# Two-sided mixers: the first output projection moved ahead of the ninth pair's scores, ten warm-up products for eight, and a small load moved ahead of the first weights

## What is computed

```python
for l in range(DEPTH):                      # DEPTH = 2, SEQ = 256, D_MODEL = 1024
    h = rms_norm(x, ffn1_norm[l])
    x = x + 0.5 * swiglu(h, ffn1_w_gate[l], ffn1_w_up[l], ffn1_w_down[l])
    h = rms_norm(x, mix_norm[l])
    (na_q, na_k, na_v, df_q, df_k, df_v,
     gq_q, gq_k, gq_v, dl_q, dl_k, dl_v) = split_in_proj(h @ w_in[l])
    ...
    o = jnp.concatenate([o_a, o_b, o_c, o_d], axis=-1)
    x = x + o @ w_out[l]
    h = rms_norm(x, ffn2_norm[l])
    x = x + 0.5 * swiglu(h, ffn2_w_gate[l], ffn2_w_up[l], ffn2_w_down[l])
```

## Time and profile before

| | us |
|---|---|
| median of 3 runs (lowest to highest) | 1570.04 (1569.96 to 1570.6) |
| the profiled execution, its own time | 1568.18 |
| its span, first to last instruction | 1566.1 |
| PE busy | 1550.7 (99%) |
| DVE busy | 1099.9 (70%) |
| ACT busy | 963.5 (62%) |

### The profile page before, as it was taken

How to read it: one execution, slowest core, us unless ns; L and a number is a source line. 1 busy time by engine, 2 the same in 40 slices (tenths; PEclk the granted TensorE clock), 3 DMA queues, 4 the chain that set the end, 5 groups by cost and what they waited for, 6 DMA issues and landing times.

```text
span 1566.1 us, 22052 instructions
## 1 busy us (share of the span) xinstructions
PE 1550.7 (99%) x7808; PEld 1292.7 (83%) x7808; DVE 1099.9 (70%) x1884; ACT 963.5 (62%) x1856; POOL 158.1 (10%) x251
## 2 busy tenths in 40 slices
PE   9999999999999999999999999999999999999998
PEld 7888888788888888888788888998788889878886
DVE  7678688777766777678777677767655477585553
ACT  7555588655555555487765555776555577675552
POOL 0010022010000000011110000012001010110100
PEclk9999999999999999999999999999999999999999
DMA  9999743389977999773269996633776656067670
GB/s 347 312 326 334 216 170 130 99 300 286 297 268 209 306 284 298 253 190 120 88 211 309 311 277 209 215 122 127 239 217 194 188 168 241 31 210 250 198 222 33
DMA packets 149516, 344.74 MB, mean 220 GB/s; under 512 B 66848, under 2 KB 67616, under 8 KB 148896
## 3 DMA queue, kind: packets, MB, share of 16 engines
q1 hardware_dynamic: 130416, 290.25, 58.4%
q10 hardware_dynamic: 18992, 53.09, 11.1%
HBM read 329.64 MB, written 1.06 MB: 211 GB/s over the span
## 4 chain that ended last, share of the span: by engine, by line
PE 94%; DVE 2%; ACT 1%; POOL 1%; DMA 1%; issue 1%; SPq 0%; DVEq 0%; POOLq 0%; ACTq 0%
PE PS L1034 27%; PE PS L1036 27%; PE PS L1035 27%; PE PS L1215 2%; PE PS L1236 2%; PE PS L1278 1%; PE PS L1376 1%; PE PS L1377 1%; PE PS L1378 1%; PE PS L1052 1%; DMA raw<-in_ffn 1%; PE PS L1258 1%; POOL st L2431 1%; PE PS L1112 0%; PE PS L1313 0%
## 5 line engine op out<-in xcount | busy, mean ns | idle before, releaser
L1917 DVE TENSOR_TENSOR Wl<-raw,Wh 128x1024 fp32r<-128x1024 f32 (+3 forms) x360 | 355.5, 1030 | 28.6 <-ACT Wh L1514 26.4
L1514 ACT ACTIVATE Wh<-raw 128x1024 fp32r<-128x1024 f32 (+3 forms) x360 | 308.7, 900 | 30.2 <-PE PS L1036 22.9
L1034 PE MATMUL PS<-Wh,Hh 128*128 128x512 f32 (+1 forms) x824 | 321.9, 391 | 1.9 <-DVE Hl L1977 1.7
L1036 PE MATMUL PS<-Wh,Hl 128*128 128x512 f32 (+1 forms) x824 | 318.9, 387 | 0.0
L1035 PE MATMUL PS<-Wl,Hh 128*128 128x512 f32 (+1 forms) x824 | 318.7, 387 | 0.0
L1917 DVE TENSOR_TENSOR QTl<-raw,QTh 128x1024 fp32r<-128x1024 f32 (+3 forms) x236 | 232.3, 1022 | 20.8 <-ACT QTh L1514 19.6
L1514 ACT ACTIVATE QTh<-raw 128x1024 fp32r<-128x1024 f32 (+3 forms) x236 | 201.8, 892 | 16.5 <-PE PS L1036 14.0
L1034 PE MATMUL PS<-QTh,Hh 128*128 128x512 f32 (+2 forms) x536 | 208.9, 390 | 0.1
L1036 PE MATMUL PS<-QTh,Hl 128*128 128x512 f32 (+2 forms) x536 | 206.4, 385 | 0.0
L1035 PE MATMUL PS<-QTl,Hh 128*128 128x512 f32 (+2 forms) x536 | 206.4, 385 | 0.0
L1599 ACT ACTIVATE WK<-PS,st 128x256 f32<-128x256 f32 x88 | 41.7, 474 | 255.5 <-PE PS L1036 254.5
(11 more groups left out here) (239 smaller groups left out, 2361.7 us busy)
## 6 DMA issues: line engine op xcount, KB each, us to landing
raw<-in_ffn SPq DMA_DIRECT2D x392, 512.0 KB, 5.4
BT<-in_ada ACTq DMA_DIRECT2D x96, 512.0 KB, 5.0
raw<-in_win SPq DMA_DIRECT2D x64, 512.0 KB, 4.8
raw<-in_wo SPq DMA_DIRECT2D x32, 512.0 KB, 5.4
raw<-in_win SPq DMA_DIRECT2D x8, 420.0 KB, 4.4
raw<-in_lat SPq DMA_DIRECT2D x6, 512.0 KB, 6.1
raw<-in_ffn SPq DMA_DIRECT2D x8, 256.0 KB, 5.7
BT<-in_nab SPq DMA_DIRECT2D x2, 1024.0 KB, 7.7
```

The source lines that it names most:

```text
L1034: e.matmul(out_, xh, wh, start=start, stop=False)
L1036: return e.matmul(out_, xl, wh, start=False, stop=stop)
L1514: ins = e.activation(high(p)[:, cc], raw[p % RAW][:, cc], ACT.Copy)
L1917: ins = e.tensor_tensor(low(p)[:, cc], raw[p % RAW][:, cc], high(p)[:, cc].bitcast(f32), ALU.subtract)
```

## The change

There are three edits. In both "a" mixers the six matmuls of `wo` chunk 0 for the first 128 positions stand ahead of pair 8's scores (eight matmuls), right behind pair 5's values. At the start SP issues the load of SM ahead of the first half piece of weights. And PE runs ten products of zeros where it ran eight.

```diff
-                ("S", 8, 0, 0), ("wo", (0,), 0, 0), ("wo", (1,), 0, 0), ("wo", (2,), 0, 0), ("T", 6, 0, 0),
+                ("wo", (0,), 0, 0), ("S", 8, 0, 0), ("wo", (1,), 0, 0), ("wo", (2,), 0, 0), ("T", 6, 0, 0),
...
+            e.dma_start(SM[:, 0:8], d["small"][:, 0:8]).then_inc(sm0_in, 16)
             half_piece(0, 0)
-            e.dma_start(SM[:, 0:8], d["small"][:, 0:8]).then_inc(sm0_in, 16)
             half_piece(0, 1)
...
-                for _ in range(8):
+                for _ in range(10):
                     e.matmul(PS[:, 7, :], ZW[:, 0:128], ZW[:, :], start=True, stop=True)
```

## The result

| | us |
|---|---|
| before, median of 8 runs (lowest to highest) | 1570.0 (1568.42 to 1572.14) |
| after, median of 8 runs (lowest to highest) | 1573.67 (1572.66 to 1578.46) |
| ratio after / before, 95% interval | 1.0031 (1.0022 to 1.004) |
| the profiled execution of after, its own time | 1578.46 |
| its span | 1576.3 |

The change makes the kernel about 0.3% slower. The direction of the central forecast was right, but the size is outside the range: the medians differ by 3.7 us where 1.5 were forecast, and the time lies above the range's upper end. The profiled execution of after is the slowest of its eight, so what it shows is more than the median has.

What follows compares the result with a forecast made beforehand. PE's list was taken to bound the kernel: 1570.04 us before plus 1.47 for the waits in the two mixers and 0 for the start gives 1571.5 us, range 1569.5 to 1573.0.

Steps and rivals of the forecast that it cites:

- central forecast: Whole kernel: 1571.5 us, 0.09% slower than before; chance 0.70 for 1571.0 to 1572.2.
- The waits: Both "a" mixers: moved projection waits for pair 5's low part, 0.73 us later in each, 1.47 us for both.
- the prediction's upper bound: Each mixer: 0.84 us later if the first product after the gap also waits for its weights.
- its extra 0.11: First product after the gap in each mixer: added time for loading its weights, 0.11 us.
- the 0.73 is neither given back nor multiplied: PE behind each mixer's pause: later waits shift with PE, so the 0.73 us reaches the end unchanged.
- rival (3): Both mixers: the longer gap makes the clock fall, 1.8 us for each, 1575.1 us in all; chance 0.04.
- Who is late behind it: Behind the moved projection: pair 8's maxima stay covered by 0.8 us, pair 6's turn shifts 0.73 with PE; no extra cost.
- The start: Warm-up and small load at program start: cost and gain 0, between -0.05 and +0.45 us; first real product at 5.94.

Runs made afterwards that it cites:

- e1: Kernel before with the reordering in both mixers alone, start unchanged; median 1573.72 us, ratio 1.0031 to before.
- e9: Kernel before with the reordering, plus three products of zeros in the pause ahead of the moved projection; median 1570.77 us, ratio 1.0001.
- e3: Kernel before with the reordering, plus seven products of zeros in the pause ahead of the moved projection; median 1571.07 us, ratio 1.0009.
- e5: Kernel before in its old order, plus four products of zeros in the pause ahead of pair 8's scores; median 1568.44 us, ratio 0.999.
- e4: Kernel before in its old order, with pair 8's scores also made to wait for pair 5's outputs; median 1574.55 us, ratio 1.003.
- e2: Kernel before with the two start edits alone (small load first, ten products of zeros), no reordering; median 1569.89 us, ratio 0.9999.
- e10: e7 with the two start edits added; median 1566.99 us, ratio 0.9981 to before.
- e7: Kernel before with only chunk 0's three bank 0 products ahead of pair 8's scores, without the s_o wait, operand made earlier; 1567.02 us, ratio 0.9983.
- e6: Kernel before with the reordering, ACT's copy and DVE's low part of pair 5's outputs put earlier in their lists; median 1569.97 us, ratio 1.0002.

## Why the prediction was wrong, point by point

**The waits: right in place and kind, but the term of the sum is too small by a third or more.** The prediction put the moved projection behind DVE's line 2128, with line 1215 no longer waiting, and a pause of 1.93 us; it is 2.04. DVE's row ends at 277.74 + 0.42 = 278.16 and PE starts at 278.42, so the release takes 0.26 and not 0.15. The start is 2.04 - 1.20 = 0.84 later by that, which is the number of the prediction's upper bound, by luck: its extra 0.11 stood for a weight load and not for the release. The rest of the term was missing: the matmuls of the scores and those of the projection do not follow each other at the plain pace. From the last projection product to the scores it is 0.33 (770.88, read from e1's timeline, to 771.21) instead of 0.23, and from the first projection product to the second 0.31; the prediction counted such a step once where there are now two. Per mixer it is 1.04 (8.61 - 7.57), for which 0.73 with an upper bound of 0.84 had been given. For both mixers it is 2.1 instead of 1.47; the medians of the kernels without a fall say 2.3 to 2.6 (e9 and e3 against e5), and what makes up the difference of 0.2 to 0.5 stays open.

**The clock: this is the step that failed, a term put at nothing.** The sentence "the 0.73 is neither given back nor multiplied" left the clock out, and rival (3), which named the right mechanism, got a chance of 0.04 and a price for both mixers at once. In the profiled execution both mixers had the fall, and it cost 3.1 and 4.4 us (11.75 and 12.98 less 8.61) where the rival had 1.8 for each; in most executions it is less, so the median moved by 3.7 us and not by the rival's 5.1. The ground for the small chance was one reading: behind the 1.20 us pause of the profiled execution the products were at once 0.23 apart. One execution can't show how often a thing of chance happens. There was a sign in the numbers at hand, and the prediction even wrote it down: the median was 1.9 us above the profiled execution. e5 explains that gap: 1568.44 with the pauses filled, close to the profiled 1568.18. So the times of before already held falls of the clock, which went when its 1.20 us pauses were filled, and a change that made these pauses longer could well have more of them: all eight executions of after, all eight of e1 and all six of e4 have a mean clock under 0.999, against 54 of the 80 of before in the three groups.

The Trainium skill's page "TensorE: Matmul & The Clock Gate", section "HAM oscillation — how this bites in real kernels", has the mechanism, an engine that waits for its inputs and is throttled again. The trace agrees with that, at a granted clock of 0.50 from 279.9 to 286.7 us. The waits in the page's case are longer, some 3 to 5 us, and for DMAs; here 2.04 us of waiting for DVE were enough.

**The medians, summed.** Without falls the kernel before is at 1568.4 (e5) and the reordering at 1570.8 to 1571.1 (e9, e3), which is 2.3 to 2.6 for the waits. With its falls before is at 1570.0, 1.6 more; the change with its falls is at 1573.7, 2.6 to 2.9 more. The difference of 3.7 is 2.3 to 2.6 from the waits and 1.0 to 1.3 from the clock. The prediction had 1.47 and 0 for them. With the waits right and no clock it would have said 1572.3 to 1572.6, with the clock alone right 1572.5 to 1572.8, both still inside its range; it took the two errors together to leave it.

**Who is late behind it.** Right: pair 8's maxima and pair 6's turn caused no wait of PE; the distance of 8.61 us is the same with (e3) and without (e1's second mixer) the filling products, and the later waits in PE's table are those of before.

**The start.** Right, at 0 (e2 and e10), but for partly wrong reasons. Timeline of PE at the start of after, answering to the earlier trace rows, and of ACT, answering to the earlier trace rows:

```profile
1.44 4.63 PE L1059 MATMUL PS<-ZW 128*128 128x512 f32 x10 [1.44 <-DVE ZW L2327]
5.87 0.69 PE L1070 MATMUL PS<-Wh,Hh 128*128 128x512 f32 x1
6.35 0.61 PE L1073 MATMUL PS<-Wh,Hl 128*128 128x512 f32 x1
6.78 0.42 PE L1076 MATMUL PS<-Wl,Hh 128*128 128x512 f32 x1
7.03 0.40 PE L1070 MATMUL PS<-Wh,Hh 128*128 128x512 f32 x1
```
```profile
4.21 0.51 ACT L1575 ACTIVATE Hh<-WK,SM 128x256 fp32r<-128x256 f32 x1 [1.28 <-DMA WK<-in_xt]
5.02 0.63 ACT L1577 ACTIVATE Wh<-raw 128x512 fp32r<-128x512 f32 x1 [0.29 <-DMA raw<-in_ffn]
```

ACT begins at 4.21 behind x, as forecast, but then waits for the later half piece of weights until 5.02 (forecast 4.8). The first real product is at 5.87 (5.94) and the fourth at 7.03 (6.85, in the range that went to 7.29). In e10 the clock rose already among the ten products: they took 3.98 us in all and the first real one came at 5.56. No cost or gain of this is seen at the end. The prediction took the moment at which the clock rises as fixed, and it isn't: in e1 and e4, whose start is that of before, the products are still 0.43 apart at 9.3 us, where in before they are 0.24 apart from 6.60 on. The recorded clock doesn't show this (in after it reads 1.00 from 2 to 4 us, where the products are 0.45 apart), so it isn't a matter of the page's rounding either. By line 1112 the executions differ by more than the edits could give: its first row is at 23.0 in before, 23.85 in after, and at 24.34 and 24.45 in e1 and e4.

## What to carry to other kernels

Before work is moved into a pause, read the waits that it brings along, in the lists of the engines that raise them: what was covered by the work in front of it becomes the wait that ends last, and often only a part of the moved work needs it (e7 moved that part alone, with one entry of DVE's list put earlier for it, and won; what each of the two is worth by itself was not run). A pause of TensorE, where it is the engine that bounds the kernel, can cost more than its length, since the clock may fall behind it, and only in some executions; compare the mean granted clock of many executions, and be warned when the profiled one is faster than the median. To find out, fill the pause with products of zeros: where the wait ends when it did, what that wins is the clock's share.

## What the runs showed of the hardware that was not expected

- The granted clock fell to 1.2 GHz (0.50) behind pauses of 2.04 us. In e1 the same pause had it in one mixer and not in the other. That it also fell behind pauses of 1.20 us, in some executions and not in others, is inferred from the times and mean clocks of before and e5; no trace shows it.
- It need not fall in the pause: in after's first mixer it fell at 279.9, 1.5 us after PE had started again, and in the second at 768.0, inside the pause.
- The stretches at 1.2 GHz differ in length: 3.4 us (e4), 6.8 us and 10.2 us (after). They cost 1.6 us (10.03 less 7.57 and less the 0.84 by which the pause is longer), 3.1 (11.75 - 8.61) and 4.4 us (12.98 - 8.61).
- Three products of 512 columns ahead of a pause of 1.15 us went with a clock that stayed up in eleven executions of eleven (e9), where with a pause of 1.13 us without them (e6) it stayed up in six of eleven.
- Switching PE between the projection's products and the scores' costs about 0.1 us each time (0.33 us to the next start instead of 0.23, e1).
